# The causal depthwise convolution of a decoder layer: one VectorE operation for each tap in place of two

## The reference, cut to what matters

```
u = a * jax.nn.sigmoid(g)
u_ext = jnp.concatenate([conv_left.astype(u.dtype), u], axis=1)
c = _causal_depthwise(u_ext, conv_w, conv_b)
c = jax.nn.silu(_layer_norm(c, conv_ln_g, conv_ln_b))
```

## Time and profile before

| | |
|---|---|
| median of 3 runs | 1510.5 us (1510.26 to 1511.56) |
| the profiled execution | 1508.58 us |
| its span, first to last instruction | 1506.8 us |
| TensorE busy | 1418.5 us, 94% |
| VectorE busy | 661.9 us, 44% |
| GpSimd busy | 495.8 us, 33% |
| ScalarE busy | 312.3 us, 21% |
| mean granted TensorE clock | 0.968 |

### The profile page before, as it was taken

The page is one execution under the profiler, slowest core; times in us unless marked ns, Lnnn a source line. Parts: engine busy times, 40 slices in busy tenths (PEclk is TensorE's granted clock), DMA queues, the critical chain, the costliest instruction groups (busy, mean ns, idle before and its releaser), DMA issues.

```text
span 1506.8 us, 22479 instructions
## 1 busy us (share of the span) xinstructions
PE 1418.5 (94%) x9063; PEld 1326.7 (88%) x9063; DVE 661.9 (44%) x1191; ACT 312.3 (21%) x707; POOL 495.8 (33%) x348
## 2 busy tenths in 40 slices
PE   6997699999999789969999999999999999999999
PEld 6997677777877556969999999999999999999998
DVE  5797743554654464558513131313131313232224
ACT  5211432432433323334310001010101010101000
POOL 1224721321321412243354424243342433424220
PEclk9998898999999879989999999999999999999999
DMA  7123221332321610100962141014111401231102
GB/s 219 54 61 113 78 89 59 111 98 81 115 86 53 221 68 3 41 28 15 321 212 69 43 154 55 28 56 139 56 42 42 167 28 56 84 111 43 47 0 119
DMA packets 50514, 130.49 MB, mean 87 GB/s; under 512 B 14336, under 2 KB 26496, under 8 KB 49920
## 3 DMA queue, kind: packets, MB, share of 16 engines
q1 hardware_dynamic: 44944, 95.47, 19.3%
q10 hardware_dynamic: 5504, 34.11, 6.6%
HBM read 120.09 MB, written 43.28 MB: 108 GB/s over the span
## 4 chain that ended last, share of the span: by engine, by line
PE 84%; DVE 7%; ACT 3%; POOL 3%; issue 2%; DMA 2%; SPq 0%; ACTq 0%; POOLq 0%; DVEq 0%
PE ps L310 24%; PE ps L311 23%; PE ps L312 23%; PE ps L747 3%; DVE uc L1194 3%; PE ps L701 2%; PE ps L763 2%; DMA raw<-in_w_stream 2%; PE ps L697 2%; PE ps L770 1%; POOL small L505 1%; PE ps L749 1%; PE ps L711 1%; PE ps L676 1%; PE ps L806 1%
## 5 line engine op out<-in xcount | busy, mean ns | idle before, releaser
L590 POOL TENSOR_TENSOR wf<-raw,small 128x1024 fp32r<-128x1024 f32 x60 | 114.1, 1902 | 429.0 <-PE ps L312 420.1
L310 PE MATMUL ps<-mh_a,wf 128*128 128x362 f32 (+1 forms) x624 | 209.0, 335 | 19.0 <-DVE y L1466 12.6
L1518 DVE TENSOR_TENSOR pr<-ps,sg 128x362 f32<-128x362 f32 (+1 forms) x66 | 35.3, 535 | 405.1 <-ACT sg L1154 405.0
L311 PE MATMUL ps<-ml_a,wf 128*128 128x362 f32 (+1 forms) x624 | 206.7, 331 | 0.0
L312 PE MATMUL ps<-mh_a,wf 128*128 128x362 f32 (+1 forms) x624 | 206.7, 331 | 0.0
L311 PE MATMUL ps<-ml_c,wf 128*128 128x362 f32 (+1 forms) x624 | 204.7, 328 | 0.0
L312 PE MATMUL ps<-mh_c,wf 128*128 128x362 f32 (+1 forms) x624 | 204.7, 328 | 0.0
L310 PE MATMUL ps<-mh_c,wf 128*128 128x362 f32 (+1 forms) x624 | 204.3, 327 | 0.0
L1194 DVE SCALAR_TENSOR_TENSOR uc<-uc,cws 128x1024 f32<-128x1024 f32 x240 | 199.9, 896 | 0.1
L1536 DVE TENSOR_TENSOR y<-ps,y 128x362 f32<-128x362 f32 (+1 forms) x264 | 139.2, 533 | 107.3 <-PE ps L312 107.3
L312 PE MATMUL ps<-ah,wf 128*128 128x364 f32 (+1 forms) x528 | 174.1, 330 | 0.0
(11 more groups left out here) (145 smaller groups left out, 2327.8 us busy)
## 6 DMA issues: line engine op xcount, KB each, us to landing
raw<-in_w_stream SPq DMA_DIRECT2D x94, 512.0 KB, 3.5
skt<-in_kT_c SPq DMA_DIRECT2D x32, 384.0 KB, 5.5
sv<-in_v_c SPq DMA_DIRECT2D x32, 384.0 KB, 5.1
xr<-in_xT SPq DMA_DIRECT2D x8, 544.0 KB, 4.5
out_yT<-y SPq DMA_DIRECT2D x8, 544.0 KB, 2.7
y<-in_xT SPq DMA_DIRECT2D x1, 2720.0 KB, 9.7
out_nv_p<-vn SPq DMA_DIRECT2D x32, 64.0 KB, 1.6
out_nk_p<-zst SPq DMA_DIRECT2D x32, 64.0 KB, 1.6
```

Of the source, the lines that this page charges most:

```text
L310: e.matmul(out, wh, mh_, start=first, stop=False)
L311: e.matmul(out, wh, ml_, start=False, stop=False)
L590: pool.tensor_tensor(hi(slot), raw[:, k % 2, :], zeros, ALU.add).then_inc(w_hi, 1)
L1518: dve.tensor_tensor(pr[:, k6 % 2, 0:bn], bank(2 * (k6 % 2) + 1, bn), sg[:, k6 % 2, 0:bn], ALU.mult).then_inc(gu_pr, 1)
```

## The change

Each tap becomes one operation over `CV` = 1328 columns, from the region's start to 30 before its end. Source and destination are contiguous. It covers the prompt's 1024 columns, the samples' 64, and 240 columns between them whose results nobody uses. The operations of all taps form one chain: each waits for the one before it (`cv_a`), and `cv_b` is gone.

```
+CV = UW - PADC
...
-        cv_a, cv_b = sem("conv_prompt"), sem("conv_samples")
+        cv_a = sem("conv_taps")
...
                     pe.wait_ge(cv_a, TAPS * CT)
-                    pe.wait_ge(cv_b, TAPS * CT)
...
                 w = cws[:, n:n + 1]
-                for s, dst, src in ((cv_a, uc[:, c * UW:c * UW + SEQ], uc[:, (c + 1) * UW + j:(c + 1) * UW + j + SEQ]),
-                                    (cv_b, ustate(c, 0, TS), ustate(c + 1, j, j + TS))):
-                    dve.wait_ge(s, n)
-                    if j == 0:
-                        dve.tensor_scalar(dst, src, w, cbs[:, c:c + 1], ALU.mult, ALU.add).then_inc(s, 1)
-                    else:
-                        dve.scalar_tensor_tensor(out=dst, in0=src, scalar=w, in1=dst, op0=ALU.mult,
-                                                 op1=ALU.add).then_inc(s, 1)
+                dst, src = uc[:, c * UW:c * UW + CV], uc[:, (c + 1) * UW + j:(c + 1) * UW + j + CV]
+                dve.wait_ge(cv_a, n)
+                if j == 0:
+                    dve.tensor_scalar(dst, src, w, cbs[:, c:c + 1], ALU.mult, ALU.add).then_inc(cv_a, 1)
+                else:
+                    dve.scalar_tensor_tensor(out=dst, in0=src, scalar=w, in1=dst, op0=ALU.mult,
+                                             op1=ALU.add).then_inc(cv_a, 1)
```

## The result

The changed kernel takes 1528.65 us (median of 4, 1523.01 to 1531.93) against 1511.03 (median of 4, 1510.26 to 1511.91): 1.0113 of the time before, 95% interval 1.0082 to 1.0143. The forecast was 1529, range 1516 to 1536, slower with 0.95. The profiled execution took 1528.59 us, its span 1526.8, 20.0 more than before.

The account below looks back on a forecast made before the run. VectorE was taken to pace the GLU groups, hand-overs the first projections, TensorE most else; terms of 15.4 us plus 3.4 for clock gave 1527.4, plus 1.9 from profiled execution to median 1529 us, range 1516 to 1536.

Parts of the forecast that it names:

- The tap: Convolution taps on VectorE: 1.59 us long, next tap 1.63 us after its start (+0.24), anything else 1.51 (+0.12).
- GLU groups: 70 to 125 us, VectorE sets the pace: four longer taps per group delay the projections' start by 5.0 us.
- the fifth group's 0.7: Fifth GLU group: its taps grow 0.83 us, less 0.15 us of VectorE idle time, so 0.7 us shows.
- Square sum and four rounds: First projections: 0.5 us before the first square sum, plus 1.7 us for each of z = 0, 2, 4, 6.
- The 0.5 for the taps ahead of the first square sum: Four taps behind the last GLU group end 0.83 us later, against 0.23 idle and 0.08 overlap: +0.5 us.
- the round of z = 0: First round of two tiles in the projections: line 511 falls behind a longer tap, +1.7 us.
- The rival that line 511 would come ahead of the tap again: Projections: z = 0 to 6 cost 4 x 0.55 = 2.2 us and no clock loss, 1521 us; chance 0.22.
- Clock: TensorE in the projections: longer waits bring two more half-clock stretches, each costing half of 3.4 us: +3.4 us.
- Behind z = 8: Three taps there end 0.8 us later, delaying line 508 and GpSimd's weight cut for the next transfer: +0.8 us.
- Attention steps: 180 to 500 us: two taps delay the samples' outputs once in each of three pairs, 1.1 us; elsewhere hidden.
- 500 to 545 us: Three tap pairs on the chain at 0.36 us each, with a little for GpSimd waiting longer: 1.2 us.
- The rest: From about 560 us on: equally long, only shifted in time, 0 us added.

Follow-up runs that it names:

- two-semaphore run: Kernel before with 1024 and 64 columns, each operation also waiting for the one just ahead through a second semaphore wait: 1518.02 us, ratio 1.0057 to before.
- the run that forces it: Changed kernel, two taps behind an odd tile's square sum in the first projections also wait for line 511 of the tile before: 1522.65 us, ratio 1.0089 to before.
- two halves: Changed kernel with each tap's 1328 columns split into two operations of 664, each with its own chain: 1518.61 us, ratio 1.0065 to before.
- both dependence runs: Kernel before, each tap operation also waiting for the one just ahead: with two semaphores 1518.02 us, with one semaphore 1510.16 us.
- the best placing: No taps in first projections, three per GLU group, 28 taps moved to attention steps: from the kernel before 1496.23 us, from the changed one 1502.11 us.
- the second filling: Changed kernel with eight unread matmuls of 512 columns ahead of the transposes of z = 2, 4, 6: 1530.12 us, ratio 1.0138 to before.

## Why the prediction was right, point by point

- **The tap.** 1.59 us long, 1.63 to a dependent successor, 1.51 to another: as taken from the earlier trace rows. By the rule of the Trainium skill that was weighed there (VectorE: DVE Perf Modes, "The DRAIN you can't avoid": the semaphore costs nothing extra) taps would start 1.51 apart; the trace of after refutes it for this operation, and the two-semaphore run shows a wait costing even more, 0.10 us after the end.
- **GLU groups.** 5.0 expected, 4.46 measured. The six groups with the start at 68.62 and later grew by 0.68 to 0.75 us each, 4.37 in sum; the prediction's terms for them, with the 0.4 taken off for GpSimd's cut, make 4.35. What was too high is the fifth group's 0.7: the sixth starts only 0.09 later than before. In the fifth VectorE had waited 0.53 us for the sigmoid, which it no longer does (before, then after):
```profile
62.28 0.54 DVE L1235 TENSOR_TENSOR uc<-glu_a,glu_s 128x362 f32<-128x362 f32 x1 [0.53 <-ACT glu_s L964]
```
```profile
61.74 0.54 DVE L1234 TENSOR_TENSOR uc<-glu_a,glu_s 128x362 f32<-128x362 f32 x1
```
- **Projections.** Square sum and four rounds were 7.3 us without the clock; measured are 6.0. The rounds of z = 2, 4, 6 cost 1.75 each, as replayed (1.75, and twice 3.31 less the 1.56 of a clock stretch). The two terms about z = 0 had another mechanism than was said. The 0.5 for the taps ahead of the first square sum did not show, since the matmuls at half clock came later still. And the round of z = 0 cost 0.75, not 1.7: line 511 stood behind a tap there already before (133.85 behind 133.70 in the earlier trace rows, which the prediction reads but does not use), so nothing changed places; three GpSimd operations only grew, by 0.32 (504), 0.25 (506) and 0.19 us (512). The rival that line 511 would come ahead of the tap again (1521 us) did not occur, and the run that forces it shows its price for the stage. That the loss is order at the shared port and not VectorE's time is shown by three runs with as much VectorE time for a tap or more (two halves, both dependence runs) that lose nothing or gain there. The rule of the Trainium skill (SBUF — State Buffer, "Who interferes with whom") that the pair is held for a whole instruction agrees with the trace: line 506 ends 0.87 us after the tap, whether the tap is 1.28 or 1.60 us long.
- **Clock.** Two more stretches expected, three came: 1.56 each, 4.7 us. With the 1.0 at the start of the projections, for which the prediction had no term, that makes 5.7 in place of 3.4: this term was low. The wait of 3.05 us, forecast as 3.0, was right.
- **Behind z = 8.** 0.8 expected, 0.96 measured.
- **Attention steps.** 1.1 expected, 0.33 measured. In the second step of a pair the square sum in front of the samples' outputs already waited for ScalarE: the outputs that stood at 309.69 stand at 326.92, 17.23 later, where the step's values (297.35 and 314.42) are 17.07 later; 0.16 of a tap pair's 0.36 comes through. What covered the rest was that wait, which the prediction left out. TensorE waits for the samples' outputs twice in these steps, 0.5 us in all. Stretches at 0.50 fall elsewhere in the two traces, so more than this can't be read.
- **500 to 545 us.** 1.2 expected, 0.61 measured. The three tap groups add 0.9 (the first, at 541.27 after 524.10, is 17.17 later, the fill behind the third 18.09), near the 1.1 expected for them; 0.3 are won back between the values and the first group, which was not traced.
- **The rest.** 0 expected, 1.9 measured, so the sign that all would be equally long from 560 us on did not hold. 1.5 of it come in the 0.50 stretch after 610 us (the lag is 18.07 at 610.21 and 19.64 at 640.02), of which the table by stretches shows the part that was at full clock before, 18.1 us earlier:
```profile
615.20:617.40 2.20, 2.20 (x8) 1.33 (x6) 1.34 (x4) 1.46 (x3) 0.00 (x0) 0.50 0.00 0
```
```profile
597.10:599.30 2.20, 2.20 (x24) 1.66 (x22) 1.30 (x3) 2.18 (x6) 0.29 (x1) 1.00 0.00 0
```
The first line is of after, the second of before. Why this stretch is longer was not tried, and where the last 0.4 come stays open.

The median came out within 1 us because errors cancelled: rounds and square sum 1.3 too high, steps and the last taps 1.4, GLU groups 0.5; clock 2.3 too low, the rest 1.9, behind z = 8 0.2. That leaves the span 1.2 us above the sum. The 1.9 us between profiled execution and median, carried over from before, made up for it: after, the two differ by 0.06. The places named were the right ones but for the start of the projections and the rest, and the main mechanism, line 511 behind a tap for z = 2, 4, 6, is the one replayed; the closeness of the total is luck.

## What to carry to other kernels

Merging two operations saves one fixed cost, but it can put work that nobody reads into the stream (240 columns, 0.25 us here), and, if the two belonged to alternating chains, it takes away the partner that hid each other's dependence (0.12 us). Before merging, look at who shares a port or a queue with the operation: the length of one instruction is the time another engine can be shut out, and a small operation of that engine on the path pays for it in full. Where such work is divided by hand over stages, moving it out of the stages whose hand-overs set the pace is worth more than its form: 15 us here, against 6 for the form at the best placing. The stages that take the work in have a limit of their own: with three taps in nearly every step the longer form cost 6.8 us there, with two 1.8.

## What the hardware showed that was not expected

- A chain that leaves short gaps can be faster than one that leaves none: with every operation waiting for the one ahead, VectorE's taps took 17% longer and the projections 5 us less, because GpSimd got in between (line 505: 1.05 us in place of 2.12). The whole kernel was not told apart from before.
- An instruction that waits for two semaphores started 0.10 us after the end of the one ahead, with one semaphore 0.04.
- With 24 or 44 matmuls added to TensorE's program ahead of its loop, the loop had four pauses, 3.4 to 3.5 us in sum, with nothing in the profile that ends them. Single executions of three other variants had one such pause each (1.2 to 1.6 us). The cause stays open.
- The time of one and the same kernel moved between 1501 and 1515 us with the mean granted clock between 0.976 and 0.964. In the changed kernel TensorE ran at 0.50 for 5.3 us behind its wait of 10.4 us for glu_a; in the second filling, behind the same wait, the first 5.4 us had a mean of 0.59.
